# Odd layer of a two-layer trunk: half of the stick-breaking projections and all latents run between attention units; weight tiles reordered; only used columns split

## The chip, the cores and the metric

The kernel runs on one core of one Trainium2 chip. The metric is the device time of one execution in microseconds. The kernel before took 1295.44 us (median of 3 runs, 1293.87 to 1296.08). About 0.2% of that, 2.6 us, is what a measurement of this kernel can tell from no change.

## The reference, cut to what matters

The program is a two-layer decoder trunk on 512 tokens of width 1024, all in float32, with a gated MLP (d_ff 2816) after each mixer. The change touches the mixer of the odd (second) layer only:

```python
c_q, c_kv, c_kr, d_q, d_k, d_v = split_cols(h @ w_in, (384, 256, 32, 512, 512, 512))
q = (rms_norm(c_q, q_norm_g) @ w_uq).reshape(b, s, 4, 96)       # last 32 of each head rotated
kv = (rms_norm(c_kv, kv_norm_g) @ w_ukv).reshape(b, s, 4, 192)  # 64 of k, 128 of v
k = concat([k_nope, rotated c_kr for every head])
o_c = mla_attention(q, k, v_c)                  # 4 heads of 96, causal softmax
o_d = stick_breaking_attention(d_q, d_k, d_v)   # 4 heads of 128, strictly causal
o = concat([o_c, o_d]); return o @ w_out
# stick breaking, per block of 128 queries:
z = q k^T * scale
log_keep = where(mask, log_sigmoid(-z), 0)
a = exp(z + log_keep + reverse_exclusive_cumsum(log_keep)); out = a @ v
```

## The kernel before, in words

**Arithmetic.** Each float32 product is made of three TensorE (PE) matmuls of rounded parts (`PASSES`): high x high, high x low, low x high. The high part of a weight tile (128 x 2048) is written by ScalarE (ACT, L366, `w_hi`), the low part by GpSimd (POOL, L288, `w_lo`, four pieces of 512 columns). The tiles come in one fixed order through two slots. A tile is loaded by SP once the low part of the tile two before it is made, its high part is written once PE is through with that tile (`split_after`, a wait on `mm_done`), then POOL makes the low part, and PE waits for it (`w_lo_ready`).

**Order of the work.** Every engine has its own written-out list of instructions and waits on semaphores, so the position in the list is the schedule. In the odd layer PE does, in this order: four tiles of q and k of the D heads (`W_DQK`, 192 matmuls of 512 columns, `first_tile` and `channels`), two tiles of v (`W_DV`, `tokens_tile`), and then a loop over n = 0 to 18 (L1598 and on) in which 16 attention units are run. A unit is one head and one block of 128 queries, and its keys are 128, 256, 384 or 512 wide. Units 0 to 7 are heads 0 and 1 with widths rising; units 8 to 15 are heads 2 and 3 with widths falling. In turn n PE makes the scores of unit n (L1607, L1609), then fill work, then the transposes of unit n-2 (L1623), then the values of unit n-3 (L1631). For one unit ACT makes Abs, Exp and Ln (L669 to L671), VectorE (DVE) a maximum-add, a scan and a subtraction (L1089, L1093, L1096), and ACT the final Exp (L675), DVE the copy of the transposes (L1122).

**Fill work before.** Turns 0 to 9 hold the latents c_q and c_kv of four token blocks (`latent`, L1555), turns 10 to 12 their transposes (`turn_latent`, L1567), turns 13 and 14 the product with w_uq (`up_q`, L1578), turns 15 to 18 the product with w_ukv (`up_kv`, L1592). In turns 10 and 11 ACT also has two high parts of 2048 columns. The subtraction L1096 writes into `probs`, from which PE transposes, so that it waits for the transposes of unit n-2 (`d_turned`), which stand behind the fill work of turn n.

**After the loop** come the two groups of attention C (`attention_c`, groups 8 and 9, two heads each): 16 transposes of q and k (L1405), eight units with softmax, and between them the early half of the output projection (`early_product`, L1276, pieces f = 0 to 7, 12 matmuls each) and the transposes for it (`early_turn`, L1254). Then the late half, the norm and the MLP follow, as in the first layer.

**PSUM** has 8 banks. Units use banks 0 to 3, fill work banks 4 and 5, values 6 and 7.

## Time and profile before

| | |
|---|---|
| median of 3 runs | 1295.44 us (1293.87 to 1296.08) |
| the profiled execution | 1295.93 us |
| its span, first to last instruction | 1294.1 us |
| mean granted TensorE clock | 0.992 of full |
| PE busy | 1238.7 us (96%), 6372 matmul records |
| weight loads (PEld) | 1061.0 us (82%) |
| DVE, ACT, POOL busy | 508.8, 495.0, 573.0 us |
| DMA | 114.76 MB, mean 89 GB/s |

The 40-slice line of PE reads 9 in all slices but five: 5 in the first, 8, 7 and 8 in the three from 744 to 841 us, and 6 in the last. The granted clock reads 9 everywhere but in two slices (8), that from 809 to 841 us and the last. The odd layer's mixer lies from about 680 to 900 us.

### The profile page before, as it was taken

To read this page: it belongs to the slowest core of one execution; us is meant where nothing else is said; L and a number is where in the kernel's file an instruction comes from. 1 tells how busy PE (TensorE), PEld (TensorE's weight loads), DVE (VectorE), ACT (ScalarE), POOL (GpSimd) and SP (SyncE) were. 2 spreads that over 40 slices of the span, in tenths; PEclk is the share of its full clock that TensorE was granted. 3 is DMA by queue.
4 is the path that set the end of the run, shared out by engine and by line. 5 is a ranking of instruction groups with operands and counts; after the bars stand their busy time and mean duration, and the time that the engine had idled before them with its cause. 6 is when DMAs were issued, how large, how long until landed. Compare 5 with 4: busy or idle time off the path is not lost.

```text
span 1294.1 us, 17224 instructions
## 1 busy us (share of the span) xinstructions
PE 1238.7 (96%) x6372; PEld 1061.0 (82%) x6376; DVE 508.8 (39%) x885; ACT 495.0 (38%) x698; POOL 573.0 (44%) x495
## 2 busy tenths in 40 slices
PE   5999999999999999999999987899999999999996
PEld 5999989888888888888878876777888888888885
DVE  6655677755222221232342148543512122132324
ACT  4455544544323232433332256243522223243332
POOL 1344344423444444466644432421344444456662
PEclk9999999999999999999999999899999999999998
DMA  7211111113222222222223211201222222222221
GB/s 269 99 67 65 65 66 66 66 66 105 76 97 96 98 96 97 97 98 97 98 70 119 96 73 39 78 33 52 96 97 97 97 97 97 97 71 102 92 93 66
DMA packets 17037, 114.76 MB, mean 89 GB/s; under 512 B 1888, under 2 KB 2016, under 8 KB 4064
## 3 DMA queue, kind: packets, MB, share of 16 engines
q1 hardware_dynamic: 16128, 110.99, 23.6%
q10 hardware_dynamic: 864, 3.15, 0.8%
q8 instruction: 31, 0.51, 0.2%
q14 instruction: 14, 0.11, 0.0%
HBM read 112.03 MB, written 2.10 MB: 88 GB/s over the span
## 4 chain that ended last, share of the span: by engine, by line
issue 42%; POOL 32%; PE 17%; DVE 6%; ACT 2%; DMA 0%; POOLq 0%; DVEq 0%; ACTq 0%
POOL w_lo L288 31%; PE ps L1309 7%; PE ps L1555 2%; PE ps L1352 2%; PE ps L1336 1%; PE ps L1492 1%; PE ps L1299 1%; DVE w_lo L744 1%; PE ps L1578 1%; DMA w_raw<-weights 0%; PE ps L1365 0%; PE ps L1366 0%; ACT tmp L409 0%; PE ps L1276 0%; DVE region L770 0%
## 5 line engine op out<-in xcount | busy, mean ns | idle before, releaser
L288 POOL TENSOR_TENSOR w_lo<-w_raw,w_hi 128x512 fp32r<-128x512 f32 x332 | 465.0, 1432 | 538.2 <-ACT w_hi L366 538.2
L366 ACT ACTIVATE w_hi<-w_raw 128x2048 fp32r<-128x2048 f32 x101 | 193.2, 1913 | 357.0 <-PE ps L1237 177.3
L1237 PE MATMUL ps<-hT_hi,w_hi 128*128 128x512 f32 x720 | 280.1, 389 | 0.0
L1237 PE MATMUL ps<-hT_hi,w_lo 128*128 128x512 f32 x720 | 280.1, 389 | 0.0
L1237 PE MATMUL ps<-hT_lo,w_hi 128*128 128x512 f32 x720 | 280.1, 389 | 0.0
L1237 PEld LDWEIGHTS ps<-hT_lo,w_hi 128*128 128x128 f32 x720 | 135.2, 188 | 28.2
L1237 PEld LDWEIGHTS ps<-hT_hi,w_hi 128*128 128x128 f32 x720 | 135.2, 188 | 27.9
L1237 PEld LDWEIGHTS ps<-hT_hi,w_lo 128*128 128x128 f32 x720 | 135.2, 188 | 27.9
L973 DVE TENSOR_TENSOR hT_lo<-region,hT_hi 128x2048 fp32r<-128x2048 f32 (+1 forms) x22 | 58.5, 2668 | 144.4 <-ACT hT_hi L576 144.4
L943 DVE SCALAR_TENSOR_TENSOR qk<-ps,vec,qk 128x511 f32<-128x511 f32 x44 | 33.0, 750 | 202.9 <-ACT qk L550 202.9
L550 ACT ACTIVATE qk<-ps,vec 128x512 f32<-128x512 f32 x44 | 34.3, 780 | 178.4 <-PE ps L1237 166.3
L1462 PE MATMUL ps<-w_hi,hT_hi 128*128 128x512 f32 x256 | 99.6, 389 | 0.0
L1462 PE MATMUL ps<-w_lo,hT_hi 128*128 128x512 f32 x256 | 99.6, 389 | 0.0
L1462 PE MATMUL ps<-w_hi,hT_lo 128*128 128x512 f32 x256 | 99.6, 389 | 0.0
L953 DVE TENSOR_TENSOR region<-ps,qk 128x512 f32 (+1 forms) x44 | 30.4, 691 | 155.4 <-PE ps L1237 155.4
L315 POOL TENSOR_TENSOR tmp<-region,cst 128x256 f32<-128x256 f32 x30 | 23.4, 781 | 145.4 <-DVE region L827 117.6
L1309 PE MATMUL ps<-w_hi,hT_hi 128*128 128x384 f32 x224 | 80.6, 360 | 1.4 <-ACT region L473 0.9
L1309 PE MATMUL ps<-w_hi,hT_lo 128*128 128x384 f32 x224 | 75.2, 336 | 0.0
L1309 PE MATMUL ps<-w_lo,hT_hi 128*128 128x384 f32 x224 | 74.0, 336 | 0.4 <-DVE w_lo L744 0.4
L1352 PE MATMUL ps<-region,xn 128*128 (+2 forms) x400 | 56.5, 273 | 0.5 <-ACT xn L492 0.5
L1462 PEld LDWEIGHTS ps<-w_lo,hT_hi 128*128 128x128 f32 x256 | 48.1, 188 | 10.1
L1462 PEld LDWEIGHTS ps<-w_hi,hT_hi 128*128 128x128 f32 x256 | 48.1, 188 | 9.9
(205 smaller groups left out, 2123.0 us busy)
## 6 DMA issues: line engine op xcount, KB each, us to landing
w_raw<-weights SPq DMA_DIRECT2D x101, 1024.0 KB, 4.8
gain<-gains ACTq DMA_DIRECT2D x5, 512.0 KB, 3.6
out<-region SPq DMA_DIRECT2D x4, 512.0 KB, 2.6
x<-x_in SPq DMA_DIRECT2D x3, 512.0 KB, 10.9
cst<-consts SPq DMA_DIRECT2D x1, 640.0 KB, 12.7
x<-x_in ACTq DMA_DIRECT2D x1, 512.0 KB, 6.6
region<-masks SPq DMA_DIRECT2D x1, 384.0 KB, 13.4
vec<-vectors SPq DMA_DIRECT2D x1, 282.5 KB, 13.0
```

The costliest lines, as they stand in the source:

```text
L288: ins = pool.tensor_tensor(w_lo[:, slot, cols], w_raw[:, slot, cols], w_hi[:, slot, cols].bitcast(f32), ALU.subtract)
L315: own.mark(pool.tensor_tensor(t1, src, cos, ALU.mult))
L366: sc.activation(w_hi[:, slot, :], w_raw[:, slot, :], ACT.Copy).then_inc(w_hi_ready, 1)
L550: sc.activation(qk[:, s, :], ps[:, s, :], ACT.Identity, scale=vec[:, ds(8 * i + (col + 2), 1)], bias=vec[:, ds(8 * i + (col + 3), 1)]).the ...
L943: own.link(ve.scalar_tensor_tensor(qk[:, s, 1:SEQ], ps[:, s, 0:SEQ - 1], vec[:, ds(8 * i + (col + 1), 1)], qk[:, s, 1:SEQ], ALU.mult, ALU. ...
L953: ve.tensor_tensor(act[:, ds(2 * i + s, 1), :], ps[:, 2 + s:3 + s, :], qk[:, 2 + s:3 + s, :], ALU.mult).then_inc(val_bank_free[l], 1)
L973: ve.tensor_tensor(hT_lo[:, places, :], act[:, ds(kt, count), :], hT_hi[:, places, :].bitcast(f32), ALU.subtract).then_inc(act_lo[l], count)
L1237: ins = pe.matmul(bank, w[:, slot, k * pitch + 128 * s:k * pitch + 128 * s + 128], h[:, k:k + 1, :], start=k == 0 and n == 0, stop=k == KT ...
L1309: ins = pe.matmul(ps[:, bank, 0:384], h_[:, 4 * half + k, t * 128:(t + 1) * 128], w_[:, half, k * 384:(k + 1) * 384], start=first and k == ...
L1352: ins = pe.matmul(o, probsT[:, m, b * 128:(b + 1) * 128], v, start=b == 0, stop=b == i)
L1462: ins = pe.matmul(ps[:, 4 * c + t, :], a[:, t * 128:(t + 1) * 128], w[:, slot, u * 512:(u + 1) * 512], start=first and u == units[0] and n ...
L1555: ins = pe.matmul(ps[:, 4 + j % 2, 0:width], h[:, k, t * 128:(t + 1) * 128], w[:, (n + part) % 2, col:col + width], start=k == 0 and m == ...
```

## The change

- Weight tiles are in a new order and cut in another way: one tile now holds q and k of one D head. Heads 0 and 1 come first, then v, then heads 2 and 3 (`W_D23`), then the latents. The number of tiles is the same.
- PE makes only q and k of heads 0 and 1 and v ahead of the loop. The other 96 matmuls of 512 columns (`d_project`, 32 steps of 3) run in turns 0 to 6. The latents move from turns 0 to 9 to turns 7 to 15. The loop has 16 turns.
- The latents' transposes, `up_q` and `up_kv` run after the loop, each with other PSUM banks (`C_BANK`, `UQ_BANK`, `UKV_BANK`), between the transposes and values of the last units. Then all `early_turn`, the transposes of q and k for group 8 (`turn_heads`) and the output piece f = 0 follow, ahead of the first unit of attention C. In attention C the pieces stand at units 2, 4, 7 and at the end of group 8, and at units 3 and 6 of group 9.
- The subtraction of a unit writes into its own sums (`d_sums`); ACT's Exp moves them to `probs` and takes over the wait for the transposes.
- q is scaled by ACT directly from PSUM, k is copied by DVE (`d_query`, `d_key`); before, DVE copied both and ACT scaled q from SBUF.
- High parts in the loop are cut in two pieces of 1024 columns (tiles `W_D23 + 1` and `W_C`), and for three tiles only the used columns are split: 1440, 1152 and 1536 of 2048. The low part of tile `W_UQ` is made by DVE.
- The two inverse roots (of c_q and c_kv) are made apart. POOL rotates q block by block (4 x 4 instructions of 128 columns or less) in place of 4 instructions for all.

The list of PE matmuls has the same shapes and counts in both kernels (3727 entries with the loops written once); only their order differs.

```diff
-        D_FILL = {0: (("q", 0, (0,)), ("q", 1, (0,))), 1: (("q", 0, (1,)), ("q", 1, (1,))), 2: (("q", 2, BOTH),),
-                  3: (("q", 3, BOTH),), 4: (("kv", 0, (0,)), ("kv", 1, (0,))), 6: (("kv", 0, (1,)),),
-                  7: (("kv", 1, (1,)),), 8: (("kv", 2, BOTH),), 9: (("kv", 3, BOTH),)}
-        D_TURN = {10: (0, 1), 11: (2, 3), 12: (4,)}
-        D_UQ = {13: (0, 1), 14: (2, 3)}
-        D_UKV = {15: 0, 16: 1, 17: 2, 18: 3}
+        D_PROJECT = {0: (0, 5), 1: (5, 10), 2: (10, 15), 3: (15, 20), 4: (20, 24), 5: (24, 28), 6: (28, 32)}
+        D_FILL = {7: (("q", 0, (0,)),), 8: (("q", 1, (0,)),), 9: (("q", 0, (1,)), ("q", 1, (1,))), 10: (("q", 2, BOTH),),
+                  11: (("q", 3, BOTH),), 12: (("kv", 0, (0,)), ("kv", 1, (0,))), 13: (("kv", 0, (1,)), ("kv", 1, (1,))),
+                  14: (("kv", 2, BOTH),), 15: (("kv", 3, BOTH),)}
...
-                    if n >= 2:
-                        ve.wait_ge(d_turned, n - 1)
-                    ve.tensor_tensor(probs[:, m, 0:w], ps[:, m, 0:w], sp_, ALU.subtract).then_inc(d_arg, 1)
+                ve.tensor_tensor(sp_, ps[:, m, 0:w], sp_, ALU.subtract).then_inc(d_arg, 1)
+                if n in (4, 7):
+                    d_key(2 + n // 7)
...
+            def d_project(a, b):
+                for step in range(a, b):
+                    block, k = step // 8, step % 8
+                    tile = W_D23 + block // 2
+                    if k == 0:
+                        if block % 2 == 0:
+                            pe.wait_ge(w_lo_ready, tile + 1)
+                        pe.wait_ge((dv_copied, dv_copied, d_q, d_k)[block], (1, 2, 3, 3)[block])
+                    col = 256 * k + 128 * (block % 2)
+                    for n, (h, w) in enumerate(PASSES):
+                        ins = pe.matmul(ps[:, 4 + block % 2:5 + block % 2, :], w[:, tile % 2, col:col + 128], h[:, k:k + 1, :],
+                                        start=k == 0 and n == 0, stop=k == KT - 1 and n == 2)
+                    if k == KT - 1:
+                        ins.then_inc(mm_done, 2)
...
+            turn_latent(0)
+            d_turn(14)
+            d_values(13)
+            turn_latent(1)
+            turn_latent(2)
+            d_turn(15)
+            d_values(14)
+            turn_latent(3)
+            turn_latent(4)
+            up_q(0)
+            d_values(15)
+            for t in range(1, NT):
+                up_q(t)
+            for t in range(NT):
+                up_kv(t)
+            for t in range(NT):
+                early_turn(1, t)
+            pe.wait_ge(kv_scaled, NT)
             pe.wait_ge(c_roped, 2)
-            pe.wait_ge(kv_scaled, NT)
-            pe.wait_ge(d_out, 8)
+            turn_heads(8, 0)
+            early_product(1, W_OUT1, 4, 0, 2)
+            turn_heads(8, 1)
...
-            split_range(W_OUT0 + 2, W_UKV + 1)
+            split_range(W_OUT0 + 2, W_C + 2)
+            split_lo(W_C + 2, (W_C + 2) % 2, 1440, 480)
+            pool.wait_ge(w_lo_ready, W_UKV)
+            split_lo(W_UKV, W_UKV % 2, 1536)
```

ACT's list, at units 10 to 12 of the kernel before (L669 to L671 are Abs, Exp, Ln of a unit, L675 the Exp of the unit before, L683 the high parts of the transposed latents):

```order
L683 ACTIVATE hT_hi<-ps,vec 128x512 x2
L398 ACTIVATE sd<-var 128x8
L399 ACTIVATE sd<-sd 128x8
L366 ACTIVATE w_hi<-w_raw 128x2048
L669 ACTIVATE tmp<-ps 128x384
L670 ACTIVATE tmp<-tmp 128x384
L671 ACTIVATE tmp<-tmp,ones 128x384
L675 ACTIVATE xn<-xn 128x384
L683 ACTIVATE hT_hi<-ps,vec 128x512 x2
L366 ACTIVATE w_hi<-w_raw 128x2048
L669 ACTIVATE tmp<-ps 128x256
```

ACT's list in the changed kernel, from the end of the loop (L689 is now the Exp of a unit, L671 the high parts of the latents, L374 the pieces of weight tiles, L666 the squares of c_kv):

```order
L689 ACTIVATE xn<-stage 128x128
L666 ACTIVATE region,ss<-region 128x256
L374 ACTIVATE w_hi<-w_raw 128x1152
L689 ACTIVATE xn<-stage 128x128
L671 ACTIVATE hT_hi<-ps,vec 128x512 x3
L666 ACTIVATE region,ss<-region 128x256
L374 ACTIVATE w_hi<-w_raw 128x1536
L671 ACTIVATE hT_hi<-ps,vec 128x512 x2
L408 ACTIVATE sd<-var 128x4
L409 ACTIVATE sd<-sd 128x4
L369 ACTIVATE w_hi<-w_raw 128x2048
```

The high parts of the latents and the whole tiles no longer stand between the Abs, Exp and Ln of units 10 to 12, but behind the last unit.

PE's list, at turns 11 and 12 of the kernel before (L1623 transposes and L1631 values of a unit, L1567 the transposes of the latents, L1607 scores):

```order
L1607 MATMUL ps<-region,qk 128x384
L1609 MATMUL ps<-mask_bf,ident_bf 128x128
L1623 MATMUL ps<-cst,xn 128x128 x4
L1631 MATMUL ps<-region,xn 128x128 x4
L1567 MATMUL ps<-cst,region 128x128 x8
L1607 MATMUL ps<-region,qk 128x256
L1609 MATMUL ps<-mask_bf,ident_bf 128x128
L1623 MATMUL ps<-cst,xn 128x128 x3
```

PE's list in the changed kernel, behind the last latent (L1685 transposes and L1696 values of a unit, L1646 the transposes of the latents, L1657 `up_q`):

```order
L1685 MATMUL ps<-cst,xn 128x128 x2
L1696 MATMUL ps<-region,xn 128x128 x2
L1646 MATMUL ps<-cst,region 128x128 x4
L1685 MATMUL ps<-cst,xn 128x128
L1696 MATMUL ps<-region,xn 128x128 x2
L1646 MATMUL ps<-cst,region 128x128 x8
L1685 MATMUL ps<-cst,xn 128x128
L1696 MATMUL ps<-region,xn 128x128
L1646 MATMUL ps<-cst,region 128x128 x8
L1657 MATMUL ps<-w_hi,hT_hi 128x384
```

The turns 10 to 12, which had no long fill work, are gone; the transposes of the latents follow a loop that has fill work in every turn.

POOL's list in the changed kernel, from the last tile of the latents to the rotation of q's first block (L290 the low parts, L343 to L348 the rotation of the shared key, L354 to L357 that of q, the latter four times):

```order
L290 TENSOR_TENSOR w_lo<-w_raw,w_hi 128x480 x3
L290 TENSOR_TENSOR w_lo<-w_raw,w_hi 128x512 x3
L343 TENSOR_TENSOR region<-region,cst 128x128
L344 TENSOR_TENSOR region<-region,cst 128x4x16
L345 TENSOR_TENSOR region<-region,cst 128x4x16
L346 TENSOR_TENSOR region<-region 128x4x32
L348 COPY region<-region 128x16x32
L354 TENSOR_TENSOR region<-region,cst 128x128
L355 TENSOR_TENSOR region<-region,cst 128x4x16
L356 TENSOR_TENSOR region<-region,cst 128x4x16
L357 TENSOR_TENSOR region<-region 128x4x32
```

The low part of tile `W_OUT1` stands behind all of these on POOL, and PE now asks for it ahead of attention C, no longer at its fourth unit.

## Rows read from the trace of the kernel before

**Rows 1.** Busy time by stretch: PE, PEld, DVE, ACT, POOL, then granted clock, DMA share, GB/s.

```profile
745.50:795.90 50.40, 46.34 (x299) 41.70 (x298) 29.14 (x52) 29.38 (x63) 10.82 (x8) 1.00 0.13 47
795.90:807.50 11.60, 4.23 (x30) 3.01 (x28) 9.38 (x15) 9.97 (x18) 7.59 (x6) 0.93 0.05 9
807.50:817.60 10.10, 8.80 (x35) 8.12 (x36) 6.09 (x10) 2.30 (x5) 5.34 (x8) 0.57 0.52 199
817.60:839.60 22.00, 17.12 (x106) 15.82 (x105) 12.05 (x28) 6.22 (x11) 9.07 (x8) 1.00 0.13 48
839.60:895.90 56.30, 54.40 (x328) 43.72 (x328) 24.20 (x51) 25.33 (x63) 9.95 (x8) 1.00 0.11 38
```

**Rows 2.** PE's longest waits from 745 to 896 us: total, times, longest.

```profile
PE ps L1631 <- DVE xn L1122: 8.5, 3, 5.1
```

**Rows 3.** PE's timeline: first of 18 matmuls and the next group, twice.

```profile
812.69 0.66 PE L1578 MATMUL ps<-w_hi,hT_hi 128*128 128x384 f32 x1 [1.26 <-DVE hT_lo L1129]
...
817.47 0.27 PE L1623 MATMUL ps<-cst,xn 128*128 128x128 f32 x1
...
819.07 0.45 PE L1578 MATMUL ps<-w_hi,hT_hi 128*128 128x384 f32 x1 [0.16 <-DVE region L1107]
...
822.33 0.27 PE L1623 MATMUL ps<-cst,xn 128*128 128x128 f32 x1
```

**Rows 4.** PE's timeline: first of 144 projection matmuls, and the next group.

```profile
691.09 0.40 PE L1237 MATMUL ps<-hT_hi,w_hi 128*128 128x512 f32 x1
...
723.75 0.39 PE L1227 MATMUL ps<-w_hi,hT_hi 128*128 128x512 f32 x1
```

**Rows 5.** PE's timeline: first of 8 latent transposes, and the next group.

```profile
794.87 0.38 PE L1567 MATMUL ps<-cst,region 128*128 128x128 f32 x2
...
795.75 0.49 PE L1607 MATMUL ps<-region,qk 128*128 128x384 f32 x1
```

**Rows 6.** ACT's and DVE's timeline: Abs and subtraction of a 512 and a 384 unit.

```profile
788.13 0.60 ACT L669 ACTIVATE tmp<-ps 128x512 f32<-128x512 f32 x1 [2.30 <-PE ps L1609]
792.17 0.69 DVE L1096 TENSOR_TENSOR xn<-ps,stage 128x512 f32<-128x512 f32 x1
793.40 0.49 ACT L669 ACTIVATE tmp<-ps 128x384 f32<-128x384 f32 x1 [2.33 <-PE ps L1609]
796.71 0.56 DVE L1096 TENSOR_TENSOR xn<-ps,stage 128x384 f32<-128x384 f32 x1
```

**Rows 7.** ACT and DVE groups by form (count, busy, mean ns, idle before), 740 to 900 us.

```profile
L366 ACT ACTIVATE w_hi<-w_raw 128x2048 fp32r<-128x2048 f32 x8 | 15.3, 1908 | 23.7 <-PE ps L1592 8.6 <-PE ps L1227 7.9 <-PE ps L1276 5.1
L1129 DVE SCALAR_TENSOR_TENSOR hT_lo<-ps,vec,hT_hi 128x512 fp32r<-128x512 f32 x5 | 3.5, 741 | 0.0
L1077 DVE COPY region<-ps 128x512 f32<-128x512 f32 x3 | 2.1, 692 | 6.1 <-PE ps L1227 6.1
L738 DVE SCALAR_TENSOR_TENSOR rs_a<-rs_a,var 128x8 f32<-128x8 f32 x1 | 1.2, 1191 | 0.0
L484 ACT ACTIVATE xn<-ps,neg_max 128x128 f32<-128x128 f32 x4 | 1.5, 368 | 2.9 <-DVE neg_max L852 2.9
```

**Rows 8.** DVE's low parts of whole tiles, in the first layer.

```profile
L744 DVE TENSOR_TENSOR w_lo<-w_raw,w_hi 128x2048 fp32r<-128x2048 f32 x18 | 41.9, 2326 | 0.0
```

**Rows 9.** POOL groups by form, 740 to 900 us.

```profile
L288 POOL TENSOR_TENSOR w_lo<-w_raw,w_hi 128x512 fp32r<-128x512 f32 x32 | 41.4, 1324 | 101.4 <-ACT w_hi L366 101.4
L352 POOL TENSOR_TENSOR region<-region,cst 128x512 f32<-128x512 f32 x1 | 1.3, 1287 | 11.3 <-DVE region L1107 11.3
L341 POOL TENSOR_TENSOR region<-region,cst 128x128 f32<-128x128 f32 x1 | 0.8, 835 | 0.0
L346 POOL COPY region<-region 128x512 f32<-128x512 f32 x1 | 0.6, 611 | 0.1
L344 POOL TENSOR_TENSOR region<-region 128x128 f32<-128x128 f32 x1 | 0.5, 460 | 0.1
L342 POOL TENSOR_TENSOR region<-region,cst 128x64 f32<-128x64 f32 x1 | 0.3, 315 | 0.0
```

More of the change, by code:

```diff
@@ new lines, in _ @@
+                if n == 13:
+                    inverse_root(0, 4)
+                if n == 15:
+                    sc.wait_ge(mm_done, 4 * (W_C + 2))
+                    split_piece(W_UQ, 0, 1152, True)
+            for c in range(3):
+                turned_high(c)
+            square_latent(7)
+            sc.wait_ge(latent_sum, 8)
+            split_piece(W_UKV, 0, 1536, True)
+            for c in range(3, 5):
+                turned_high(c)
+            inverse_root(4, 8)
+            split_after(W_UQ)
@@ new lines, in _ @@
+            split_lo(W_UQ, W_UQ % 2, 1152)
+            copy_turned(14)
+            for c in range(3):
+                turned_low(c)
+            copy_turned(15)
+            copy_out(12)
+            ve.wait_ge(c_squared, 8)
+            variance(4, 8, 1.0 / 256)
+            for c in range(3, 5):
+                turned_low(c)
+            copy_out(14)
+            for t in range(NT):
+                ve.wait_ge(mm_done, 4 * (W_C + 2) + 2 * t + 2)
+                ve.tensor_scalar(q_tok[:, t, :], ps[:, UQ_BANK[t], 0:384], rstd[:, t:t + 1], None, ALU.mult)\
+                  .then_inc(q_scaled, 1)
+                if t == 0:
+                    refine(4, 8)
@@ L1131, in _ @@
+            for t in range(NT):
+                half_low(8 + t + 1, O_BANK[t], 4, t)
             for g in (8, 9):
@@ new lines, in d_values @@
+            def d_values(n):
+                p, i, m, w = d_unit(n)
+                if n == 0:
+                    pe.wait_ge(dv_copied, NT)
+                pe.wait_ge(d_copied, n + 1)
+                if m == 0 and n >= 4:
+                    pe.wait_ge(d_out, (n - 2) // 2)
+                for b in range(i + 1):
+                    ins = pe.matmul(ps[:, 6 + n // 2 % 2, 128 * m:128 * m + 128], probsT[:, m, b * 128:(b + 1) * 128],
+                                    dv[:, b, 256 * p + 128 * m:256 * p + 128 * m + 128], start=b == 0, stop=b == i)
+                ins.then_inc(d_pv, 1)
```

388 lines of the change are left out of this document (202 added, 186 removed).

## The prediction

> **What bounds the kernel now.** I read the page first: PE is busy for 96% of the span and its weight loads for 82%, so time can come only from work taken off PE or from PE's idle time. The change takes no matmul away (the lists have the same shapes and counts), so it is worth what it gives back of PE's waits, and nothing more. Then I read the busy time by stretch, from the first attention unit (745.5 us) to the end of attention C (895.9 us) [rows 1]. The reader is to see that PE is idle for 50.4 - 46.34 = 4.1, 11.6 - 4.23 = 7.4, 10.1 - 8.80 = 1.3, 22.0 - 17.12 = 4.9 and 56.3 - 54.40 = 1.9 us, together 19.5 us of 150.4. The list of waits names the largest cause: the values of a unit wait for DVE's copy of its transposes, 8.5 us in three waits and 5.1 us in one [rows 2]. That one is at turn 12, where PE has no fill work and ACT has two whole tiles and four latent parts in its list. Last the clock: it is granted at 1.00 up to there, 0.57 after that long wait and 1.00 again later [rows 1], that is at the lower level, 1.2 GHz, for most of a 10 us stretch.
>
> **The price of the low clock.** Eighteen matmuls take 817.47 - 812.69 = 4.8 us in that stretch and 822.33 - 819.07 = 3.3 us behind it [rows 3]: 1.5 us lost. From the end of the long wait to the next one PE does some 3.9 us of work at the low level, of which half is lost, 1.9 us. Together 3.4 us. The granted clock as a check: 0.43 x 10.1 = 4.3 us, part of it over idle time. So at most 19.5 + 3.4 = 22.9 us can come back.
>
> **Ahead of the loop** nothing changes for PE: 96 of 192 matmuls are moved into turns 0 to 6 at the same (723.75 - 691.09) / 144 = 0.227 us each [rows 4], 21.8 us in all. The copies of q and k stand beside them and hold no one back. I cost this at nothing; its cover is that a tile needs 1.9 us on ACT and 4 x 1.3 us on POOL [rows 7, 9] and PE's tile before it lasts 48 x 0.227 = 10.9 us.
>
> **What PE still waits for.** A matmul of 384 columns costs 3.3 / 18 = 0.18 us [rows 3], one of 512 0.227, a transpose of 128 columns (795.75 - 794.87) / 8 = 0.11 [rows 4, 5], and the values of one block twice that, an estimate. A unit's chain from Abs to the subtraction takes 792.17 + 0.69 - 788.13 = 4.7 us at 512 keys and 796.71 + 0.56 - 793.40 = 3.9 us at 384 [rows 6]. I add 0.2 us for handoffs and the tail of PE's last matmul.
>
> (a) Turn 5: block 3 of the new projections goes to the bank that DVE empties (k of head 2) behind the chain of unit 4. Chain 3.9 + copy 0.7 [rows 7] + 0.2 = 4.8 us. PE meanwhile has 12 x 0.227 = 2.7 of projections, 0.4 of transposes and values, 0.7 of scores: 3.8. Wait 0.9 us.
> (b) Turn 8: the latent waits for the copy of k of head 3 behind the chain of unit 7. 4.7 + 0.7 + 0.2 = 5.6, against 15 x 0.18 = 2.7, then 1.0 and 0.9: 4.6. Wait 1.0 us.
> (c) Turn 10: the third latent waits for DVE's copy of the first, behind unit 9's chain: 5.6 against 18 x 0.18 = 3.2, 1.3 and 0.7. Wait 0.3 us.
> (d) Behind the loop: from its last matmul DVE has four small copies (1.6, an estimate from 0.69 for 512 columns), the low part of `W_UQ` (1152 of 2048 columns at 2.33 [rows 8], 1.3) and three low parts of the latents (3 x 0.7 [rows 7]), together some 4.9 us, less the overlap of neighbours, 4.7. PE has 20 transposes (2.2) and the last units' 1.6: 3.8. `up_q` waits 0.9 us.
> (e) Tile `W_OUT1`: POOL now has, from the high part of `W_UKV`, three pieces (3.8), the shared key (0.83 + 0.31 + 0.31 + 0.46 + 0.61, with gaps 2.6), q in four blocks (4 x (0.83 + 0.31 + 0.31 + 0.46), 7.7) and four pieces (5.1) [rows 9]: 19.2 us. PE starts `up_q` 0.8 us before that high part is ready (ACT has a square and 1536 columns to do) and then has 36 and 48 matmuls at 0.18 (15.1), 24 transposes (2.7) and the last values (0.2): 18.0. So f = 0 waits 19.2 + 0.8 - 18.0 = 2.0 us. No row shows the block-wise rotation. Below: as the rotation at 512 columns, 1.29 for the first of four instructions [rows 9], some 4.2 in all, and no wait. Above: all sixteen at 0.83, 13.3 us, and 7.6 us. I take 2.0, since the shared key's instructions have the very size.
> (f) Attention C: the second head's key is copied behind f = 0 and again behind f = 4, 0.65 us of wait each; the first softmax of each group (0.37 of Exp [rows 7]) has no fill over it, 0.4 each; ACT's whole tile stands ahead of a copy late in group 8, 0.3; the last unit of group 9 has no fill, 0.5. Together 2.9, where the stretch of before had 1.9 [rows 1]. Bounds 1.5 and 5.
>
> In all other turns PE has about 4.9 us of work (2.7 of fill, 2.2 of a 512 unit), ACT under 2.7 + 1.9, and the scores' own chain has two turns. Here the Exp in place of the subtraction pays: the subtraction no longer waits for transposes that stand behind the fill. The tightest tile is the second of the latents: 9.9 us of chain against 10.2 of PE's work.
>
> **The sum.** 0.9 + 1.0 + 0.3 + 0.9 + 2.0 + 2.9 = 8.0 us of waits in place of 19.5, and no long wait that lowers the clock: 11.5 + 3.4 = 14.9 us. The profiled execution had 1295.9 us (span 1294.1 and 1.8 around it; 0.5 above the median), so I predict 1281.0 us.
>
> **The rivals.**
> *DVE and POOL block each other.* In the trace an 8-column DVE instruction with two inputs from SBUF takes 1.19 us while POOL makes low parts [rows 7], about one POOL instruction. The changed kernel has scans on DVE beside four tiles of low parts in the loop, in turns with 0.4 to 1 us to spare: one scan held for about 1.2 us at each of three tiles, 3.6 us, gives 1284.6. The Trainium skill, page SBUF — State Buffer, section SBUF: two separate sides, has the rule behind this: a DVE instruction with two SBUF inputs and a GpSimd one lock each other out for a whole instruction. By that rule, the trace agrees. Against its having much effect here: the two turns that wait in my sum have their scans when POOL is idle or nearly done. Chance 0.12.
>
> *The clock falls once more.* At f = 0 the wait of (e) is followed by 0.65 and 0.4 us and by short transposes and scores. If that does what the 5.1 us wait did, 3.4 us are lost: 1284.4. Chance 0.09. The Trainium skill, page TensorE: Matmul & The Clock Gate, section What's actually happening, says that the low level is the default and that activity releases it. For it: thin work. Against it: in attention C of before PE waited 1.0 us and the clock stayed at 1.00 [rows 1].
>
> *The gain does not come.* DVE's list in the loop grows by key copies, then three kinds of copies beside each chain. If every one of the 13 turns with fill loses about what (a) and (b) lose, 11 us more, the kernel takes 1292. Against it: the chain has two turns, 9.8 us, and DVE's own work at 512 keys is under 4 us. Chance 0.06.
>
> *Slower: the low clock holds through attention C.* That stretch has 54.4 us of PE work [rows 1] at full clock. Each microsecond of it done at 1.2 GHz costs one more. From 14.9 + 2.6 = 17.5 us of work at the low level on, the kernel is slower than before by over 0.2%; if two thirds of the stretch went so, 36 us, it would take 1317 us. It would start at f = 0. For it speaks only that the early turns are thinner than before; against it that the low clock of before ended within 10 us under such work. Chance 0.03.
>
> **How the numbers follow.** Forecast 0.70, rivals 0.12, 0.09, 0.06, 0.03. The bounds inside the forecast: (e) down to 0 and (f) down to 1.5 give 1277.6, (e) at 7.6 with the rest gives 1286.6. The range of 1276.5 to 1287 takes these in and the first two rivals, and leaves the last two out with a little of the forecast. Faster by over 0.2% (about what a measurement tells from no change, 2.6 us, that is below 1292.8): 0.95. Within 0.2%: 0.02. Slower: 0.03.
>
> **What would show it.** Right: the longest PE wait between the start of the loop and the end of attention C is at the first `early_product`, about 2 us, on POOL; waits of about 1 us on DVE's copy of k in turns 5 and 8; `up_q` waits under 1 us on the latents' low parts; the granted clock is 1.00 in all these stretches; PE's idle time there is 8 us over a stretch that begins 21.8 us earlier in the program. Wrong: waits on `w_lo` within the loop (the tile chain), scans of over 1.3 us at 512 keys in the waiting turns, a granted clock below 1, or a total of idle time above 12 us.

## The result, and the profile after

The changed kernel takes 1273.7 us (median of 4 runs, 1273.41 to 1273.94), the kernel before 1295.56 us (median of 4). The ratio is 0.983, 95% interval 0.982 to 0.985. The kernel got faster, as forecast, but the gain of 22.0 us (1295.93 to 1273.91 in the two profiled executions) is larger than the 14.9 us that I had forecast, and lies outside the predicted range.

The rows below give the busy time of the changed kernel by stretch, from the first attention unit to the late output product. The four stretches are the first units, the latents, `up_q` to the first output piece, and attention C (columns as in [rows 1]).

```profile
721.90:757.00 35.10, 34.51 (x169) 27.02 (x167) 17.76 (x32) 20.72 (x38) 10.52 (x9) 1.00 0.19 67
757.00:798.20 41.20, 40.27 (x279) 38.31 (x279) 25.64 (x51) 21.17 (x51) 9.37 (x7) 1.00 0.14 52
798.20:823.90 25.70, 24.96 (x161) 23.67 (x160) 18.72 (x35) 11.85 (x19) 18.57 (x30) 1.00 0.32 115
823.90:874.00 50.10, 48.15 (x286) 37.90 (x284) 20.43 (x45) 22.29 (x57) 8.03 (x7) 1.00 0.13 47
```

PE is idle for 0.6, 0.9, 0.7 and 2.0 us in these stretches, where [rows 1] gave 19.5, and the granted clock is 1.00 throughout. These are PE's waits in that part (total, times, longest); they answer to [rows 2]:

```profile
PE ps L1633 <- DVE region L1102: 0.8, 1, 0.8
PE ps L1657 <- DVE hT_lo L1129: 0.7, 1, 0.7
PE ps L1613 <- DVE region L1102: 0.6, 1, 0.6
PE ps L1477 <- DVE qk L946: 0.6, 1, 0.6
PE ps L1477 <- issue: 0.5, 1, 0.5
PE ps L1392 <- ACT xn L494: 0.5, 1, 0.5
```

L1613 and L1633 are the waits of turns 5 and 8 for the copies of k, L1657 is `up_q`, the rest is attention C. The 2 us that I expected ahead of the first output piece are missing. This is where the 22.0 us went, by the two timelines:

| | us |
|---|---|
| idle time of PE from the first unit to the late product, 19.5 before [rows 1], 4.2 now | 15.3 |
| low clock behind the 5.1 us wait, as the prediction prices it (1.9 + 1.5) | 3.4 |
| first layer, code that is the same in both kernels: 1.7 of low clock and 0.1 of idle time | 1.8 |
| what is left of PE's busy time (1238.7 before, 1232.1 now); an estimate gives it to restarts: behind a wait a matmul doesn't overlap the end of the one before, and there are ten waits fewer, 0.15 us each | 1.5 |

The expectation of a_again below splits the same 22.0 us a little differently (3.5 for the low clock, 1.3 for the restarts). No run separates the last line from the others.

The last two lines are ones that the prediction doesn't have. Here is the granted clock in two stretches of the first layer, before and after (same columns):

```profile
185.00:190.00 5.00, 3.81 (x27) 3.67 (x26) 1.66 (x5) 1.85 (x4) 3.14 (x5) 0.81 0.00 0
190.00:195.00 5.00, 5.00 (x32) 5.00 (x31) 3.41 (x7) 4.69 (x7) 0.00 (x0) 0.85 0.00 0
```

```profile
185.00:190.00 5.00, 3.81 (x36) 3.67 (x35) 1.83 (x5) 2.57 (x6) 3.14 (x5) 1.00 0.00 0
190.00:195.00 5.00, 5.00 (x35) 5.00 (x33) 3.42 (x10) 3.80 (x6) 0.00 (x0) 1.00 0.00 0
```

In both kernels PE waits 1.19 us at 186 us and then does thin work; in one trace the clock falls behind that wait, in the other it doesn't.

### The profile page after: what moved, and what is told of

Same layout as the page of the kernel before. It is cut to its first block, busy times and chain, and to the rows that moved or that the text cites. A ratio compares the mean times of both kernels' runs of the same rounds, so it can differ in the third digit from the quotient of the medians.

```text
span 1272.1 us, 17211 instructions
## 1 busy us (share of the span) xinstructions
PE 1232.1 (97%) x6376; PEld 1055.9 (83%) x6376; DVE 506.2 (40%) x885; ACT 494.0 (39%) x702; POOL 566.6 (45%) x501
## 4 chain that ended last, share of the span: by engine, by line
issue 38%; POOL 30%; PE 24%; DVE 5%; ACT 2%; DMA 1%; POOLq 0%; DVEq 0%; ACTq 0%
POOL w_lo L290 30%; PE ps L1365 7%; PE ps L1633 2%; PE ps L1277 2%; PE ps L1408 2%; PE ps L1613 2%; PE ps L1557 2%; PE ps L1243 1%; PE ps L1392 1%; DVE w_lo L773 1%; PE ps L1287 1%; PE ps L1355 1%; PE ps L1258 1%; PE ps L1696 1%; ACT tmp L419 1%
## 5 line engine op out<-in xcount | busy, mean ns | idle before, releaser
L290 POOL TENSOR_TENSOR w_lo<-w_raw,w_hi 128x512 fp32r<-128x512 f32 (+1 forms) x326 | 457.3, 1434 | 535.5 <-ACT w_hi L369 476.6
L369 ACT ACTIVATE w_hi<-w_raw 128x2048 fp32r<-128x2048 f32 x96 | 183.7, 1913 | 313.7 <-PE ps L1287 155.2
L1287 PE MATMUL ps<-hT_hi,w_hi 128*128 128x512 f32 x688 | 267.7, 389 | 0.0
L1287 PE MATMUL ps<-hT_hi,w_lo 128*128 128x512 f32 x688 | 267.7, 389 | 0.0
L1287 PE MATMUL ps<-hT_lo,w_hi 128*128 128x512 f32 x688 | 267.6, 389 | 0.0
L1287 PEld LDWEIGHTS ps<-hT_lo,w_hi 128*128 128x128 f32 x688 | 129.2, 188 | 27.0
L1287 PEld LDWEIGHTS ps<-hT_hi,w_lo 128*128 128x128 f32 x688 | 129.2, 188 | 26.8
L1287 PEld LDWEIGHTS ps<-hT_hi,w_hi 128*128 128x128 f32 x688 | 129.2, 188 | 26.4
L881 DVE TENSOR_REDUCE neg_max<-ps 128x1 f32<-128x128 f32 (+3 forms) x80 | 39.1, 489 | 44.0 <-PE ps L1426 20.8
```

Of the source, the lines that this page charges most:

```text
L290: ins = pool.tensor_tensor(w_lo[:, slot, cols], w_raw[:, slot, cols], w_hi[:, slot, cols].bitcast(f32), ALU.subtract)
L369: sc.activation(w_hi[:, slot, :], w_raw[:, slot, :], ACT.Copy).then_inc(w_hi_ready, 1)
L881: ve.tensor_reduce(neg_max[:, k:k + 1], ps[:, m, 0:w], AX.X, ALU.max, negate=True).then_inc(max_ready, 1)
L1287: ins = pe.matmul(bank, w[:, slot, k * pitch + 128 * s:k * pitch + 128 * s + 128], h[:, k:k + 1, :], start=k == 0 and n == 0, stop=k == KT ...
```

## The experiments

Each ratio is to the kernel before, with its 95% interval; a microsecond is 0.08%. The intervals of the changed kernel's variants are about 1.8 us wide to each side, and most variants ran on another chip than a_again. So a difference to a_again of less than that rests on the traces, whose waits repeat to 0.1 us, and not on the medians.

| run | median us (lowest to highest) | ratio |
|---|---|---|
| a_again | 1273.56 (1273.51 to 1275.8) | 0.9836 (0.9822 to 0.9849) |
| b_again | 1295.57 (one execution) | |
| b_junk | 1295.65 (1293.69 to 1296.27) | 1.0002 (0.9993 to 1.0012) |
| b_junk2 | 1293.82 (1293.01 to 1295.81) | 0.9992 (0.9983 to 1.0001) |
| b_exp | 1293.54 (1292.35 to 1294.83) | 0.9987 (0.9978 to 0.9996) |
| b_act | 1292.96 (1290.73 to 1294.37) | 0.9976 (0.9967 to 0.9986) |
| b_refine | 1296.13 (1293.97 to 1296.68) | 1.0005 (0.9996 to 1.0014) |
| b_act_refine | 1294.57 (1290.94 to 1294.85) | 0.9992 (0.9983 to 1.0001) |
| a_noexp | 1274.26 (1273.84 to 1276.34) | 0.9841 (0.9828 to 0.9855) |
| a_pool1 | 1274.99 (1274.49 to 1276.93) | 0.9845 (0.9831 to 0.9858) |
| a_lock | 1277.51 (1276.78 to 1278.36) | 0.9863 (0.9848 to 0.9878) |
| a_fullsplit | 1276.16 (1275.58 to 1277.48) | 0.9853 (0.9838 to 0.9868) |
| a_uneven | 1278.11 (1275.93 to 1278.86) | 0.986 (0.9845 to 0.9875) |
| a_keys | 1272.96 (1272.77 to 1273.39) | 0.983 (0.9817 to 0.9844) |
| a_keys_tile | 1271.57 (1271.3 to 1273.92) | 0.9814 (0.98 to 0.9827) |
| a_uq_pool | 1273.97 (1273.67 to 1275.82) | 0.9836 (0.9822 to 0.9849) |
| a_best | 1271.33 (1270.84 to 1271.56) | 0.9812 (0.9799 to 0.9826) |

**The first layer's clock: a_again and b_again, both kernels unchanged.**

> The changed kernel once more, as the base for the others. My theory of the 22.0 us by the two traces: 15.3 us of waits of TensorE in the odd layer that are gone (19.9 before, 4.5 now), 1.3 us of restarts behind those waits, 3.5 us of low clock in the odd layer, and 1.8 us of low clock at about 188 us, in the first layer, in code that the change doesn't touch. If the last is chance, it comes and goes from run to run in both kernels: single times of a kernel would differ by about 1.8 us, and this kernel gives 1273.7 or, with the drop, 1275.5. Rival: the change itself did away with it (1273.7 always, and 1295.5 always before).

> The kernel before once more, for its trace alone. My theory: its waits repeat to 0.1 us (the trace that I predicted from had 19.9 us of them in the odd layer), and falls of the clock at 188 us and in turn 5 come or go: with neither the time is 1294.0, with one 1295.5 to 1296. Rival: the trace has no such fall and still takes 1295.5, so that the spread of this kernel has another cause.

The changed kernel took 1273.5 to 1273.6 us four times and 1275.8 once, so a step of about 2 us exists there too. The trace of b_again, the kernel before at 1295.57 us, has the fall of the clock:

```profile
185.00:190.00 5.00, 3.81 (x26) 3.67 (x26) 1.54 (x4) 1.63 (x5) 3.14 (x5) 0.79 0.00 0
190.00:195.00 5.00, 5.00 (x31) 5.00 (x30) 3.53 (x8) 4.78 (x7) 0.00 (x0) 0.87 0.00 0
```

Now over all 19 traces. In the seven of the kernel before and of its variants with turn 5 unfilled, the clock falls either at 188 us (2 traces) or behind the 2.2 us wait of turn 5 (5 traces), and never at both. Of the eleven traces of the changed kernel and its variants, three have it at 188 us (a_pool1, a_fullsplit, a_keys_tile), none has one in turn 5. So the fall at 188 us is not of the change's making. But the change took the second place away: turn 5 now waits 0.6 us. Of the 21 times of the kernel before that were taken with a_again, 15 lie at 1295.0 or above and six at 1293.9 to 1294.5. Those six fit an execution without either fall, though no trace shows one. The falls do not make the miss: between the fastest executions, 1293.87 and 1273.41 us, the gain is still 20.5 us. The expectation of b_again, that the waits repeat, held: 5.1, 2.2, 1.5, 1.3 us as before.

**The price of the low clock: b_junk and b_junk2.**

```diff
+                if n == 12:
+                    for j in range(36):
+                        pe.matmul(ps[:, 6, 256:512], hT_hi[:, 7, 0:128], hT_hi[:, 6, 0:256], start=True, stop=True)
```

> The kernel before, with 36 matmuls of 256 columns put into the 5.1 us wait of turn 12; they write columns that nothing reads. It prices the low clock by itself. My theory: the wait ends when it did (no other wait is touched), the clock is granted at 1.00 behind it, and 3.4 us are saved: 1292.0. Rival: the low clock was an average over idle time and cost little (under 1 us, 1295), or the added matmuls delay the values that follow them, if they run longer than the wait (36 x 0.11 = 4.0 us at full clock).

The added matmuls kept the clock at 1.00 behind turn 12. The rows are the busy time by stretch, and PE's timeline of the first `up_q` (start, duration, and at the end the idle time and who ended it):

```profile
805.00:810.00 5.00, 4.10 (x34) 3.81 (x33) 4.90 (x8) 2.23 (x5) 5.00 (x5) 1.00 0.43 157
810.00:815.00 5.00, 2.04 (x13) 1.72 (x12) 4.43 (x8) 2.30 (x5) 3.77 (x7) 1.00 0.65 216
```

```profile
813.62 0.41 PE L1578 MATMUL ps<-w_hi,hT_hi 128*128 128x384 f32 x1 [2.96 <-DVE hT_lo L1129]
...
816.83 0.49 PE L1623 MATMUL ps<-cst,xn 128*128 128x128 f32 x3
```

Yet my 3.4 us fail. The 18 matmuls take 3.2 us and not 4.8 [rows 3], which is about the 1.5 us that I had worked out for them. The other 1.9 us do not come: the wait of `up_q` behind it is 2.96 us in place of 1.26 [rows 3]. The latents' low parts on DVE were as late as ever (both kernels need 5.15 us from the values of turn 12 to the first `up_q`), and slow PE work had only covered the wait. So, by the durations of this trace, the kernel gets back 1.6 us of low clock if nothing else changes, and all 3.4 only with the wait behind it gone, as in the changed kernel. The measured median shows not even the 1.6 us (1295.65, against 1295.2 for the kernel before taken with it). In this trace the clock fell behind turn 5's wait instead and cost 2.9 us there (from the values at 771.46 to the next transposes at 777.88, 6.4 us where before has 3.5), while the trace of before has the fall of the first layer, 1.7 us. That fits the 0.7 us between the two profiled executions; whether the other ten did the same is not shown.

b_junk2 adds 14 such matmuls at n == 5.

> The kernel before with matmuls of 256 columns, whose results nothing reads, in two waits: 36 in that of turn 12 (5.1 us), as in the run before, and 14 in that of turn 5 (2.2 us), behind which two of the three traces of that kernel and its variants showed the low clock for some 5 us. My theory now: low clock follows a wait of a microsecond or more by chance, at 188 us, in turn 5 or both, and surely after 5.1 us; each fall costs 1.6 to 2.9 us. With both waits filled the odd layer stays at 1.00 and only the fall of the first layer (1.8 us) comes and goes: a fastest time of 1292.3, a median of 1292.5 to 1294.2. Rival: the clock falls elsewhere in their place (the other waits of 1.1 to 3 us), and the median stays at 1295.2 to 1295.7, as with one filled.

Six times lie at 1293.0 to 1293.8 and five at 1295.5 to 1295.8. The median is in my range, but its interval takes in no change. The profiled execution is of the second kind. Its turn 5 and first layer are at 1.00, and the clock falls at the 2.95 us wait of `up_q`, to 0.56 and 0.76 from 810 to 820 us, where b_junk has 1.00:

```profile
810.00:815.00 5.00, 3.58 (x11) 3.61 (x12) 2.29 (x5) 0.42 (x1) 1.56 (x4) 0.56 0.55 210
815.00:820.00 5.00, 4.84 (x26) 4.51 (x26) 2.02 (x5) 1.08 (x4) 0.00 (x0) 0.76 0.01 3
```

The rival was half right: with two waits filled, the clock fell at the next one in this trace.

**What held turn 12: b_act, b_refine, b_act_refine.** I had put the 5.1 us on ACT's list.

```diff
-                if n in (10, 11):
-                    m = W_C + n - 9
+                if n in (10, 12):
+                    m = W_C + n // 2 - 4
```

> The kernel before with one item of ACT's list moved: the whole high part of the w_ukv tile, which stood in turn 11 ahead of the Abs, Exp and Ln of unit 12 and isn't asked for until turn 15, stands in turn 12. It asks what held the values of turn 12 for 5.1 us. My theory: ACT's list. The wait falls to 3.2 us, by the 1.9 us of the moved instruction; the clock still falls behind it: -1.9 us against the kernel before (1293.5). Rival: the wait is that of unit 10's own chain through VectorE, or comes from the missing fill alone, and ACT's item only shows in the list: 0.

The time came about as forecast: 2.7 us less by the medians (1.8 to 4.3 by the interval) than the kernel before taken with it, where I had expected 1.9. The waits did not: turn 12's went from 5.1 to 4.1 us, not to 3.2, and that of `up_q` from 1.3 to 0.7. What gave way is on DVE. This is its list ahead of the copy L1122 that the values wait for, in the kernel before:

```profile
803.74 0.57 DVE L737 TENSOR_TENSOR rs_a<-sd 128x8 f32<-128x8 f32 x1
804.35 1.19 DVE L738 SCALAR_TENSOR_TENSOR rs_a<-rs_a,var 128x8 f32<-128x8 f32 x1
805.57 1.19 DVE L739 SCALAR_TENSOR_TENSOR rstd<-rs_a,sd 128x8 f32<-128x8 f32 x1
806.79 0.69 DVE L1122 COPY xn<-ps 128x512 f32<-128x512 f32 x1
```

With ACT's tile moved, GpSimd had no second tile to work on at that moment, and L739 took 0.17 us. The next run therefore moves the three instructions of 8 columns behind the copy:

```diff
-                if n == 11:
-                    refine(0, 8)
...
                     ve.tensor_copy(probsT[:, m, 0:w], ps[:, 2 + m, 0:w]).then_inc(d_copied, 1)
+                if n == 11:
+                    refine(0, 8)
```

> The kernel before with one item of VectorE's list moved: the three refining instructions of the inverse roots, 128 x 8 each, stand behind the copy of unit 10's transposes, for which the values of turn 12 wait, and no longer ahead of it. In the trace of before they take 0.57, 1.19 and 1.19 us there, the last two beside GpSimd's low parts, where 0.17 us is what one takes alone (in the run with ACT's item moved). My theory now: turn 12's wait of 5.1 us is made of these 3.0 us and of ACT's list ahead of the chain; the wait falls to 2.2 us, and the kernel gains 2.9 us (1292.7), and less if the refining then delays the next unit's chain. Rival: the values wait for ACT's order in truth, the copy stands where it stood: 0 to -0.5.

> The kernel before with both items moved, VectorE's refining behind the copy and ACT's high part of the w_ukv tile one turn later. My theory: the two shares of turn 12's wait are mostly apart (4.1 us was left with ACT's item moved, of which the refining is 1.9), so that 2.2 us are left with both or with VectorE's alone, and the second item adds only what it takes off the waits behind it: 1292 to 1292.7. Rival: the shares add, -1.6 and -2.9 to 4.5 us (1291.2).

These are PE's waits from 797 to 824 us in b_refine, then in b_act_refine:

```profile
PE ps L1631 <- DVE xn L1120: 3.2, 2, 2.0
PE ps L1567 <- DVE hT_lo L1129: 2.7, 1, 2.7
```

```profile
PE ps L1631 <- DVE xn L1120: 3.2, 2, 2.0
PE ps L1567 <- DVE hT_lo L1129: 1.6, 1, 1.6
```

The 5.1 us became 2.0, close to the 2.2 that I had expected, and nothing was won: the transposes of the fifth latent part (L1567) then wait 2.7 us for the low parts that stand behind the refining on the same engine. Both of my times for these two runs fail: b_refine is 1.0 us slower than the kernel before taken with it (1296.13 against 1295.16), b_act_refine 0.6 us faster (1294.57), and neither is clear of no change. With both edits the second wait is 1.6 us, since DVE's last two instructions are free of GpSimd:

```profile
804.28 1.21 DVE L737 TENSOR_TENSOR rs_a<-sd 128x8 f32<-128x8 f32 x1
805.53 0.17 DVE L738 SCALAR_TENSOR_TENSOR rs_a<-rs_a,var 128x8 f32<-128x8 f32 x1
805.73 0.17 DVE L739 SCALAR_TENSOR_TENSOR rstd<-rs_a,sd 128x8 f32<-128x8 f32 x1
```

So 3.0 of the 5.1 us are the refining ahead of the copy, and moving it inside DVE's list is worth nothing, since the low parts behind it are then late. The other 2.0 us I did not test. The trace of before points at ACT after all, at its first tile and not at the second, which b_act moved:

```profile
797.94 1.90 ACT L366 ACTIVATE w_hi<-w_raw 128x2048 fp32r<-128x2048 f32 x1
...
801.45 0.56 DVE L1089 SCALAR_TENSOR_TENSOR stage<-ps,tmp 128x384 f32<-128x384 f32 x1 [1.98 <-ACT tmp L671]
```

DVE is idle for 1.98 us before its chain of unit 11, waiting for ACT's Ln, and ACT made a whole tile directly ahead of that unit's Abs, Exp and Ln. The same 1.98 us stand in b_refine and b_act_refine. That this tile costs turn 12 about 2 us is read from the trace and not shown by a run. The change takes all of this work out of a turn without fill.

**The decoupled subtraction: b_exp and a_noexp** (the hunk of L1096 and the Exp, done alone, and undone alone).

> The kernel before, with one part of the change alone: the subtraction writes into the unit's own sums, and the Exp moves them to the tile that is transposed and takes over the wait for the transposes. My theory: the waits of before come from ACT's and VectorE's lists in turns 10 to 13 and from missing fill, so this part alone gives 0 to 1.5 us (1294 to 1295.5). Rival: the coupling was a main cause, and undoing it alone gives 5 us or more (1290).

> The changed kernel without that part: the subtraction again writes the tile that is transposed and waits for the transposes of the unit before the last. My theory: those transposes stand behind the fill of turn n, about 3 us into it, and the key copies of turns 5 and 8 stand behind the subtraction on VectorE; Exp comes later by 1 to 2 us per unit and PE waits in several turns: 3 to 8 us slower (1277 to 1282). Rival: the scores' chain has two turns of slack and nothing is lost (1273.7).

Alone it gives 1.7 us by the medians (0.5 to 2.8 by the interval), near the upper end of my 0 to 1.5; in its trace PE's waits in the loop are 1.2 us shorter, all of them at `up_q` and `up_kv`. Undone it costs 0.7 us (1274.26 against 1273.56), not the 3 to 8 that I had expected: one wait of 0.2 us is new, all others are the same. That is near the rival, by which the two turns of the chain cover it.

**The fill in every turn: a_uneven.**

```diff
-        D_PROJECT = {0: (0, 5), 1: (5, 10), 2: (10, 15), 3: (15, 20), 4: (20, 24), 5: (24, 28), 6: (28, 32)}
+        D_PROJECT = {0: (0, 10), 1: (10, 16), 4: (16, 24), 5: (24, 28), 6: (28, 32)}
```

> The changed kernel with the same 32 steps of projections dealt unevenly: 10, 6, 0, 0, 8, 4 and 4 in turns 0 to 6, in place of 5, 5, 5, 5, 4, 4, 4. It asks whether it is the fill in each turn that took the waits away. My theory: turns 2 and 3 have 1 to 1.5 us of work against a unit's chain of 3 to 4 us, the values of units 0 and 1 wait for VectorE's copy 2 to 3 us in all, and turn 5's wait stays: +2 us (1275.6), more if the clock falls behind them. Rival: the chain has two turns, the long turns 0 and 1 cover it, and nothing changes: 0.

PE's waits in the turns without fill, and the stretches behind them:

```profile
PE ps L1696 <- DVE xn L1120: 2.0, 1, 2.0
PE ps L1685 <- ACT xn L689: 1.1, 1, 1.1
```

```profile
735.00:740.00 5.00, 1.95 (x7) 0.99 (x6) 3.86 (x8) 3.22 (x8) 2.19 (x2) 0.88 0.27 85
740.00:745.00 5.00, 5.00 (x19) 3.97 (x18) 2.77 (x5) 2.89 (x5) 0.00 (x0) 0.78 0.30 125
```

There are 3.1 us of new waits, and turn 5's 0.6 is gone. The fastest time is 2.4 us above a_again's median, in line with my 2. The other three are 4.3 to 5.3 above, and the trace of one of them has the low clock on top. So the same matmuls are worth 2.4 us more when they are dealt evenly, and 4.3 to 5.3 in three of four executions. This shows that fill in each turn counts. It doesn't show what the rest of the 15.3 us is made of: no run puts the latents' transposes, `up_q` and `up_kv` back into the loop, so for turns 10 to 18 the cause is read from the two timelines.

**The chain to the first output piece: a_pool1, a_lock, a_fullsplit, a_uq_pool.** GpSimd's rows of the changed kernel for one block of q, and the tile behind the fourth block:

```profile
813.55 0.46 POOL L354 TENSOR_TENSOR region<-region,cst 128x128 f32<-128x128 f32 x1
813.97 0.32 POOL L355 TENSOR_TENSOR region<-region,cst 128x64 f32<-128x64 f32 x1
814.25 0.33 POOL L356 TENSOR_TENSOR region<-region,cst 128x64 f32<-128x64 f32 x1
814.65 0.46 POOL L357 TENSOR_TENSOR region<-region 128x128 f32<-128x128 f32 x1
815.07 5.01 POOL L290 TENSOR_TENSOR w_lo<-w_raw,w_hi 128x512 fp32r<-128x512 f32 x4
```

A block takes 1.52 us, where I had priced 1.9, and the tile is ready at 815.07 + 5.01 = 820.08, 0.05 us before PE starts the piece. My 0.835 us came from [rows 9]; in that trace the instruction (810.38 to 811.21) stood beside a scan of 256 columns that took 1.47 us and not 0.69:

```profile
809.50 1.47 DVE L1093 TENSOR_TENSOR_SCAN stage<-stage 128x256 f32<-128x256 f32 x1
...
810.38 0.83 POOL L341 TENSOR_TENSOR region<-region,cst 128x128 f32<-128x128 f32 x1
```

a_pool1 adds a GpSimd instruction, a_lock four on DVE:

```diff
             split_lo(W_UKV, W_UKV % 2, 1536)
+            own.link(pool.tensor_tensor(c_tmp[:, 0, :], cst[:, 0:512], cst[:, 128:640], ALU.add))
```

```diff
             for t in range(NT):
+                ve.tensor_tensor((d_sums, tmp)[t // 2][:, t % 2, 0:512], cst[:, 0:512], cst[:, 128:640], ALU.add)
                 ve.wait_ge(mm_done, 4 * W_UKV + t + 1)
```

> The changed kernel with one more GpSimd instruction of 512 columns (two inputs from SBUF, its result is read by nobody) between the last low part of the latents' weights and the rotation. It asks how close the tile of the first output piece is. The trace of the changed kernel has that tile ready 0.05 us before TensorE is. My theory: the chain on GpSimd has no slack, so 1.2 to 1.3 us more on it are a wait of the same size ahead of the first output piece: +1.2 us against the changed kernel (1274.8). Rival: there is slack somewhere (TensorE is held by its own work, the wait falls on another's): +0.3 or less.

> The changed kernel with four VectorE additions of 512 columns, both inputs from SBUF, results read by nobody, put into VectorE's idle time while GpSimd rotates q. It asks why an instruction of the rotation took 0.835 us in the trace that I priced from and 0.46 us in the changed kernel. My theory: there it stood beside a scan of VectorE, and the two block each other; so some of the sixteen instructions here take 0.8 us or more, the rotation as a whole 1.2 to 2 us longer than 6.1, and the first output piece waits for it: +1.2 to +2 us (1275 to 1275.5). Rival: 0.835 us was a cost of the operation's shape or of its place as the first of the list, and VectorE's additions change nothing: all sixteen stay at 0.32 to 0.46 us, +0.

a_pool1 has a wait of 1.4 us ahead of the piece, and is 1.4 us slower by the medians, so the chain has no slack. In a_lock three of the sixteen instructions were held, and the wait is 2.0 us, the upper end of what I had expected. The rows are its longest PE wait, two of the held instructions with an added DVE instruction, and the stretches behind the wait:

```profile
PE ps L1333 <- POOL w_lo L290: 2.0, 1, 2.0
```

```profile
810.62 0.79 POOL L357 TENSOR_TENSOR region<-region 128x128 f32<-128x128 f32 x1
...
812.88 1.02 POOL L354 TENSOR_TENSOR region<-region,cst 128x128 f32<-128x128 f32 x1
812.90 0.68 DVE L1173 TENSOR_TENSOR stage<-cst 128x512 f32<-128x512 f32 x1
```

```profile
820.00:825.00 5.00, 3.03 (x15) 2.37 (x13) 2.23 (x4) 2.85 (x4) 5.00 (x5) 0.89 0.24 61
825.00:830.00 5.00, 4.33 (x22) 3.24 (x22) 1.87 (x4) 1.22 (x4) 2.54 (x3) 0.77 0.62 208
```

The fastest execution is 3.3 us and the profiled one 4.8 us slower than a_again, more than the wait. For the profiled one the last two rows show the clock at 0.89 and 0.77 behind it. The Trainium skill, page SBUF — State Buffer, section SBUF: two separate sides, says that whichever of the two begins first keeps the port for its whole instruction. By that rule, the trace agrees on the holding, in both directions: here GpSimd's 0.46 us becomes 1.02 beside a DVE addition of 0.68, above DVE's 0.17 us becomes 1.19 beside a GpSimd piece of 1.3. Which one began first the trace can't tell: the two rows start 0.02 us apart, GpSimd's ahead.

a_fullsplit puts 2048 in place of 1440, 1152 and 1536 columns:

> The changed kernel with one part undone: the last three tiles of the latents' weights are split over all 2048 columns again, not over the 1440, 1152 and 1536 that are used. My theory: each microsecond of it lies on a chain without slack. VectorE's low part grows by 2.33 - 1.35 = 1.0 us, all of it ahead of the first product with w_uq, and GpSimd's by one piece, 1.3 us, ahead of the first output piece; the first of these delays also takes TensorE with it, so that the second has 0.3 us left: +1.3 us in all, bounds 1.0 and 2.5 (1274.9). Rival: ACT's and GpSimd's lists have room there and only the copy work grows: under +0.3.

It is slower by 2.6 us by the medians and 2.0 at the fastest, above my 1.3 and inside my bounds at the fastest. The low part takes 2.28 us, the copy L1120 behind it on DVE holds the values of unit 14 for 1.0 us, `up_q`'s own wait stays at 0.7, and the first piece waits 0.7 us. The unused columns are worth about 2 us.

a_uq_pool moves `split_lo(W_UQ, ...)` from DVE to GpSimd, in three pieces of 384 columns:

> The changed kernel with the low part of the w_uq tile made by GpSimd, in three pieces of 384 columns, and not by VectorE. It tests term (d), the wait of up_q, and whether the chain of the first output piece has any slack. My theory: VectorE is free 1.35 us earlier, the low parts of the latents follow ACT's high parts at once, and up_q starts 0.5 us earlier; but the chain of the first output piece begins at ACT's high part of the w_ukv tile, which does not move, so that the 0.5 us come back there as a wait on GpSimd: 0 in all (1273.6). Rival: the chain has slack and the gain stays: -0.5 to -0.7 (1273.0).

`up_q` starts 0.3 us earlier against the work before it, and the first output piece now waits 0.2 us for GpSimd. There is no gain (1273.97), as expected.

**Further: a_keys, a_keys_tile, a_best.**

```diff
-                if n in (4, 7):
-                    d_key(2 + n // 7)
+                if n in (3, 6):
+                    d_key(2 + n // 6)
```

> The changed kernel with the copies of k of heads 2 and 3 one unit earlier in VectorE's list (behind the subtraction of units 3 and 6, not of 4 and 7). It tests terms (a) and (b) of the prediction, the waits of turns 5 and 8 (0.6 and 0.8 us in the trace). My theory: both go; turn 9 then asks for its weight tile 0.8 us earlier, and that tile was only just ready, so the second gain comes back as a wait there: -0.8 us in all (1272.9). Rival: both gains stay (-1.6), or the copies stand in the way of a unit's chain, and nothing is gained (0).

> The changed kernel with the key copies one unit earlier, as before, and with ACT's high part of the tile that turn 9 needs moved ahead of the Abs, Exp and Ln of unit 7. It asks whether the 1.2 us that turn 9 then waits for its tile is held by ACT's order alone. My theory: the high part is made as soon as its slot is free, GpSimd has the tile in time, and the wait of 1.2 us goes: -1.9 us against the changed kernel (1271.7). Rival: the tile is held by GpSimd (four pieces behind the tile before) or by the load, and the wait stays: -0.6 (1273.0); or ACT's whole high part delays unit 7 and the values wait for it.

> The changed kernel with everything found so far: key copies and turn 9's tile as in the run two before, the w_uq tile's low part on GpSimd, and the last 512 columns of the first output tile's low part on VectorE, in its idle time between two copies of the product with w_ukv. My theory: GpSimd's chain to the first output piece gets shorter by a piece, 1.25 us, less what the lock with VectorE costs it once, 0.3 to 0.7; that is enough for the 0.5 us that up_q gains to stay: -2.4 us against the changed kernel (1271.2). Rival: VectorE's piece holds GpSimd for a whole instruction and more, and the w_uq gain is lost: -1.9 (1271.7).

In a_keys both waits for the key are gone, and turn 9 waits for its tile, so that 0.6 us of the 1.4 are won. These are that tile on GpSimd and PE's wait for it, from the timelines:

```profile
755.91 5.93 POOL L290 TENSOR_TENSOR w_lo<-w_raw,w_hi 128x512 fp32r<-128x512 f32 x4 [5.13 <-ACT w_hi L369]
...
761.90 0.45 PE L1633 MATMUL ps<-w_hi,hT_hi 128*128 128x384 f32 x1 [1.15 <-POOL w_lo L290]
```

a_keys_tile puts `split_after(W_D23 + 1)` ahead of unit 7's Abs in ACT's list; GpSimd then starts that tile at 753.82 us, and the wait is gone: -2.0 us against a_again. a_best adds the w_uq tile on GpSimd and the last 512 columns of the first output tile's low part on DVE (three pieces stay on GpSimd): 1271.33 us, 2.2 below a_again, and its trace has no wait of PE for the tile of the first output piece. It is faster than both kernels, though most of the gain is a_keys_tile's; between those two the times don't decide.

## Why the prediction was wrong, by its own steps

- *What bounds the kernel:* right. PE's idle time and the clock gave back 20.5 of the 22.0 us, and the rest follows from the waits too, by my estimate; PE's share is now 97%.
- *The cause of the longest wait:* I named missing fill and ACT's list. Of the 5.1 us, 3.0 are three refining instructions on DVE, two of them held by GpSimd. The other 2.0 stand behind ACT's first tile in the trace, which no run tested. The sum didn't use the cause, so nothing was lost by it.
- *The price of the low clock, 3.4 us:* it fits the difference of the two kernels, but taken away alone the low clock gives back 1.6 us, by the durations of b_junk's trace.
- *Ahead of the loop, nothing:* right for the odd layer. But PE stands 1.8 us earlier there already (689.25 against 691.09 us at the layer's first matmul of 512 columns), almost all of it by the first layer's clock. I had read the granted clock only from 745 us on, and so put the clock ahead of the loop at nothing without a reason.
- *(a), (b), (c), (d):* 0.9, 1.0, 0.3, 0.9 predicted; 0.6, 0.8, 0.1, 0.7 measured. Each is 0.2 to 0.3 too large, about the 0.2 us that I added for handoffs and tails, so these four are right in place and cause.
- *(e), 2.0 us, is the term that failed:* the wait is not there. I took a duration, 0.83 us, from a single instruction that DVE was holding, and used it five times, once for the shared key and four times for q. It is 0.46 us. With it the chain on GpSimd is 17.1 us (803.02 to 820.08) and not 19.2. That PE and the tile then meet within 0.05 us is chance.
- *(f), 2.9 us:* 1.9 measured. The second key costs 0.5 and 0.6, the first softmax 0.5 once.
- *The sum:* the waits are 4.2 us and not 8.0, which is 3.8 us, of which (e) is the largest part. The restarts, 1.5 us, and the first layer, 1.8 us, were not in it at all. Together that is the 7.1 us between 14.9 and 22.0.
- *The range:* the mis-sized waits alone would have kept the result inside it. With 4.2 us of waits my own sum gives 19.5 - 4.2 + 3.4 = 18.7 us, 1277.2, and the low end was 1276.5. What put the result outside are the two terms that I had at nothing. That 22.0 comes near my upper limit of 22.9 is therefore luck: the limit counts neither of them.
- *The rivals:* the lock is real and was dear where I had not looked, in the kernel before. In the changed kernel it stretched one scan to 1.92 us and turn 9's tile to 5.9 us in place of 5.0, and that tile was just in time; with the keys earlier PE waited 1.15 us for it (a_keys). The second fall of the clock did not come, and no wait in these stretches was longer than 0.8 us. In a_lock and a_uneven, each with a new wait of 2.0 us, it did come. The rivals in which the gain fails to come, or the low clock stays, did not occur.

## What to carry to other kernels

Before a duration from one instance enters a sum, look at what the other engine did at that moment, and take another instance of the same size if there is one. Spread fill over all turns: dealt unevenly, the same matmuls left 2.5 us more waiting here. A wait that is filled or shortened alone can reappear as the next wait, as in b_junk, b_refine and a_keys. Read the granted clock of the whole span, not of the changed stretch: a fall elsewhere belongs in the baseline.
